# A decoder block in one fused kernel: first rows ahead of the constants, SSM turn factors moved into the attention, norm steps spread over the RW products, two units moved behind the gated product

## The reference

```python
def rms_norm(x, g):
    x32 = x.astype(jnp.float32)
    y = x32 * lax.rsqrt(jnp.mean(x32 * x32, axis=-1, keepdims=True) + EPS)
    return (y * g.astype(jnp.float32)).astype(x.dtype)
...
def diff_attention(q1, q2, k1, k2, v, lam):
...
        attn = probs(q1b, k1) - lam * probs(q2b, k2)
        return jnp.einsum('bhqk,bhkd->bhqd', attn, v32)
...
def s5_ssm(u, a_re, a_im, log_dt, b_re, b_im, c_re, c_im, d_skip):
```

## Time and profile before

| What | Value |
|---|---|
| Median of 3 runs | 3587.25 us (3585.57 to 3601.52) |
| Profiled execution, its time | 3581.31 us |
| Its span | 3579.3 us |
| Mean granted TensorE clock | 0.935 |
| Busy: PE, DVE, ACT, POOL | 87%, 49%, 24%, 55% |
| First product of the projection starts | 57.35 us |
| Projection ends, attention of half 0 begins | 218.5 and 243.6 us |
| glu(0) and the start of phase 1 | 548 to 604 us |
| mix_norm of half 1 in phase 2 | 1329 to 1362.7 us |

### The profile page before, as it was taken

One profiled execution on the slowest core, in us unless ns is written; L12 is line 12 of the kernel. 1 busy time (PEld: TensorE's weight loads), 2 busy tenths in 40 slices (PEclk: granted clock), 3 DMA queues, 4 the chain that ended last, 5 costly groups with the idle time before them and its releaser, 6 DMA issues.

```text
span 3579.3 us, 47875 instructions
## 1 busy us (share of the span) xinstructions
PE 3113.0 (87%) x19536; PEld 2394.1 (67%) x19536; DVE 1744.9 (49%) x2362; ACT 855.8 (24%) x1588; POOL 1969.1 (55%) x1076
## 2 busy tenths in 40 slices
PE   5977886699998768988999978988999989799997
PEld 4655564477776556766777766776777767688875
DVE  6733553443443552576666653286655564323233
ACT  3102112332222232122233223112222332200012
POOL 4801222255555464755676655665666674477873
PEclk9868997799999888999999999999999999899998
DMA  3334323122222233322222233432222221322331
GB/s 136 109 99 108 90 88 106 65 71 83 77 66 70 89 122 133 128 83 77 88 76 84 69 123 113 143 103 74 82 70 81 84 80 60 118 95 92 97 99 60
DMA packets 158027, 329.99 MB, mean 92 GB/s; under 512 B 34960, under 2 KB 74064, under 8 KB 157808
## 3 DMA queue, kind: packets, MB, share of 16 engines
q1 hardware_dynamic: 58752, 213.94, 18.6%
q10 hardware_dynamic: 99056, 112.99, 9.8%
HBM read 281.89 MB, written 44.97 MB: 91 GB/s over the span
## 4 chain that ended last, share of the span: by engine, by line
PE 71%; DVE 19%; ACT 3%; ACTq 2%; DMA 2%; issue 2%; DVEq 0%
PE ps L1778 30%; PE ps L1819 12%; PE ps L1807 12%; PE ps L1632 2%; DVE acc_dense L2219 2%; DVE ffh_lo L2903 1%; DVE act_lo L2219 1%; PE ps L1513 1%; DVE xn_dense L2226 1%; PE ps L2018 1%; ACTq L934 1%; PE ps L1553 1%; PE ps L1660 1%; DVE added L2219 1%; DVE turn L2219 1%
## 5 line engine op out<-in xcount | busy, mean ns | idle before, releaser
L537 POOL TENSOR_TENSOR w_hi<-w_raw,ones 128x1024 fp32r<-128x1024 f32 x408 | 795.0, 1949 | 1318.3 <-DMA w_raw<-weights 1304.3
L539 POOL TENSOR_TENSOR w_lo<-w_raw,w_hi 128x1024 fp32r<-128x1024 f32 x408 | 1006.6, 2467 | 32.0
L1778 PE MATMUL ps<-act_hi,w_hi 128*128 128x512 f32 x1696 | 702.6, 414 | 7.2 <-DVE act_lo L2219 6.6
L1778 PE MATMUL ps<-act_lo,w_hi 128*128 128x512 f32 x1696 | 676.7, 399 | 0.0
L1778 PE MATMUL ps<-act_hi,w_lo 128*128 128x512 f32 x1696 | 672.3, 396 | 0.0
L1778 PEld LDWEIGHTS ps<-act_hi,w_hi 128*128 128x128 f32 x1696 | 323.0, 190 | 99.1 <-issue 15.7
L1778 PEld LDWEIGHTS ps<-act_hi,w_lo 128*128 128x128 f32 x1696 | 322.8, 190 | 74.8
L1778 PEld LDWEIGHTS ps<-act_lo,w_hi 128*128 128x128 f32 x1696 | 322.8, 190 | 66.2 <-issue 1.7
L2219 DVE TENSOR_TENSOR acc_dense<-acc_dense,ps 128x512 f32<-128x512 f32 x352 | 242.0, 688 | 231.9 <-PE ps L1807 170.9
L1807 PE MATMUL ps<-w_hi,ffh_hi 128*128 128x512 f32 x704 | 293.7, 417 | 59.7 <-DVE acc_dense L2219 56.2
L1807 PE MATMUL ps<-w_hi,ffh_lo 128*128 128x512 f32 x704 | 279.7, 397 | 0.0
(11 more groups left out here) (374 smaller groups left out, 4482.9 us busy)
## 6 DMA issues: line engine op xcount, KB each, us to landing
w_raw<-weights SPq DMA_DIRECT2D x408, 512.0 KB, 3.5
rw<-rw_t ACTq DMA_DIRECT2D x24, 256.0 KB, 2.4
rw<-lora_t ACTq DMA_DIRECT2D x24, 256.0 KB, 2.0
row<-x ACTq DMA_DIRECT2D x8, 512.0 KB, 3.5
row_dense<-x ACTq DMA_DIRECT2D x8, 512.0 KB, 3.7
res<-row_dense ACTq DMA_DIRECT2D x8, 512.0 KB, 2.6
row_mix<-res ACTq DMA_DIRECT2D x8, 512.0 KB, 7.4
res<-row_mix ACTq DMA_DIRECT2D x8, 512.0 KB, 2.9
```

The costliest lines, as they stand in the source:

```text
L537: pool.tensor_tensor(w_hi[:, s], raw, ones[:, 0:1].to_broadcast([P, 1024]), MUL).then_inc(w_hi_made, 1)
L539: pool.tensor_tensor(w_lo[:, s], raw, w_hi[:, s].bitcast(F32), SUB).then_inc(w_ready, 1)
L1778: mm = pe.matmul(out, ws[w][:, s, P * k:P * k + P], acts[a][:, k, x], start=(k, w, a) == (0, 0, 0), stop=(k, w, a) == (KT - 1, 1, 0))
```

## The change

Six things change.

1. At the start ACT issues the first three rows and the gain ahead of the constants; `load_ssm` moves behind the third norm step, the lambda value and the SSM exponent behind the first norm; SP waits for the five constants before its first weight.
2. `double_frames` becomes `more_frames` and leaves the projection: three SSM steps `("frames", 0..2)` at attention steps 1, 3 and 5, the last doubling in two halves; the store is issued at the third. Attention(0)'s loads no longer wait for it, `load_input_factors(0)` does. The table and its scratch have other places in SBUF.
3. `rotated` writes its product back into PSUM, so that the third operation reads PSUM and SBUF.
4. The last two far units (nine pieces) come behind attention steps 66 and 67, behind the gated product of half 0, and their weights behind the GLU's.
5. Phase 1: the last four steps are followed by 12, 8, 4 and the rest of the chunks, four fewer ahead of them.
6. Phase 2: `mix_norm`'s six steps move out of the residual norm to behind RW tiles 0, 2, 4, 6, 8 and 10 (before: none there). Phase 3: `dense_norm`'s six steps move from behind tiles 0 to 5 to behind the same even tiles. `rw_t` and its neighbours lie 16 KB further on, off `acc_mix`.

```diff
-    SSM_STEPS = [("states", 0), ("states", 1), ("tables", 0), ("outputs", 0)]
+    SSM_STEPS = [("frames", n) for n in range(3)] + [("states", 0), ("states", 1), ("tables", 0), ("outputs", 0)]
...
-    rw_t = place("rw_t", [P, 2, BANK], F32, AT_MIX)
+    rw_t = place("rw_t", [P, 2, BANK], F32, AT_MIX + 16384)
...
-        return [ahead] + spread(through - ahead, ATT_STEPS - 1) + [8, 4, 4, rest - through - 16]
-
-    FILLS = {1: fills_heads(8, 8 * HALF + NORM_STEPS + 224, len(first_starts)),
-             2: fills([10, 8, 6, 6, 4, 4], [0] * RW_TILES, len(first_starts)),
+        return [ahead] + spread(through - ahead, ATT_STEPS - 1) + [12, 8, 4, rest - through - 24]
+
+    FILLS = {1: fills_heads(8, 8 * HALF + NORM_STEPS + 220, len(first_starts)),
+             2: fills([8, 8, 6, 6, 4, 0], [1, 0] * NORM_STEPS + [0] * (RW_TILES - 2 * NORM_STEPS), len(first_starts)),
...
-        at = [12, 14, 15] + [18 + 3 * n for n in range(2 * TB - 2)]
-        gated = (60, 63, 65, 67)
+        at = [1, 3, 5, 12, 14, 15] + [18 + 3 * n for n in range(2 * TB - 2)]
+        gated, ahead = (60, 63, 65, 67), FAR_PIECES - 9
...
+            elif n < gated[1]:
+                now = 8 + 2 * early + (ahead - 8 - 2 * early) * (n + 1 - early) // (gated[1] - early)
+            else:
+                now = min(FAR_PIECES, ahead + 5 * max(0, n - gated[2]))
...
+        sp.wait_ge(const_landed, 16 * 5)
         for pos, (_, u) in enumerate(ORDER):
...
-            if m == 0:
-                act.wait_ge(tables_stored, 16 * (3 * TB + 2))
...
         def load_input_factors(b):
+            if b == 0:
+                act.wait_ge(tables_stored, 16 * (3 * TB + 2))
...
+                elif kind == "frames":
+                    if b == 2:
+                        store_frames()
...
-                act.wait_ge(tables_stored, 16 * (3 * TB + 2))
+                act.wait_ge(tables_stored, 16 * 3 * TB)
...
+        for n in range(3):
+            load_row(0, n)
+        act.dma_start(gain_first[:, :], t["pre_mix_g"].partition_broadcast(P)).then_inc(gain_landed, 16)
         load_consts()
-        load_ssm()
+        table_for(ACT.Ln)
+        take(arg_ready)
+        first_norm()
         lambda_value()
...
-            tt(rope_sin_part[:, 0:c1 - c0], ps[:, bank, 0:c1 - c0], rope[:, 1, c0:c1], MUL)
+            tt(ps[:, bank, 0:c1 - c0], ps[:, bank, 0:c1 - c0], rope[:, 1, c0:c1], MUL)
             tt(qk_raw[:, m % 2, c0:c1], qk_raw[:, m % 2, c0:c1], rope[:, 0, c0:c1], MUL)
-            tt(qk_raw[:, m % 2, c0:c1], qk_raw[:, m % 2, c0:c1], rope_sin_part[:, 0:c1 - c0], ADD, rope_done)
+            tt(qk_raw[:, m % 2, c0:c1], ps[:, bank, 0:c1 - c0], qk_raw[:, m % 2, c0:c1], ADD, rope_done)
...
-        def double_frames(n):
+        def more_frames(have, n, first=1):
...
-                    for n in (1, 2, 4, 8, 16, 32):
-                        double_frames(n)
-                else:
-                    double_frames(64)
...
+                elif kind == "frames":
+                    for have, n, first in (((1, 1, 1), (2, 2, 1), (4, 4, 1), (8, 8, 1), (16, 16, 1)), ((32, 32, 1),), ((64, 32, 1), (64, 32, 33)))[b]:
+                        more_frames(have, n, first)
```

More of the change, by code:

```diff
@@ L194, in build @@
     turn = place("turn", [P, 2, 2, TQ, STATES], F32, ARENA + 29024)
-    frames = place("frames", [P, 2, PAIRS, STATES], F32, ARENA)
-    frame_tmp = place("frame_tmp", [P, 2, PAIRS * 64], F32, ARENA + 16640)
+    frames = place("frames", [P, 2, PAIRS, STATES], F32, ARENA + 16640)
+    frame_tmp = place("frame_tmp", [P, 2, PAIRS * 32], F32, ARENA + 12480)
     tables_at = {}
@@ L324, in build @@
     gain_post_mix = (place("gain_post_mix", [P, D], F32, AT_KEEP), gain_dense)
-    rw_t = place("rw_t", [P, 2, BANK], F32, AT_MIX)
[L327 to L331, removed]
+    rw_t = place("rw_t", [P, 2, BANK], F32, AT_MIX + 16384)
+    lora_t = place("lora_t", [P, 2, BANK], F32, AT_MIX + 20480)
+    wa = place("wa", [P, BANK], F32, AT_MIX + 24576)
+    sgd = place("sgd", [P, BANK], F32, AT_MIX + 26624)
+    lora_w = place("lora_w", [P, 4 * P], F32, AT_MIX + 28672)
+    lora_g = place("lora_g", [P, 4 * P], F32, AT_MIX + 30720)
     before_half = place("before_half", [P, RW_TILES], F32, AT_KEEP + 4096)
@@ L488, in head_events @@
         events, done, early = ["heads"] + ["far"] * 8, 8, 14
[L489 to L490 removed]
+        at = [1, 3, 5, 12, 14, 15] + [18 + 3 * n for n in range(2 * TB - 2)]
+        gated, ahead = (60, 63, 65, 67), FAR_PIECES - 9
         for n in range(ATT_STEPS - 1):
[L492 removed]
+            if n < early:
+                now = 8 + 2 * (n + 1)
+            elif n < gated[1]:
+                now = 8 + 2 * early + (ahead - 8 - 2 * early) * (n + 1 - early) // (gated[1] - early)
+            else:
+                now = min(FAR_PIECES, ahead + 5 * max(0, n - gated[2]))
             events += ["heads"] + ["far"] * (now - done) + ["ssm"] * at.count(n) + ["glu"] * gated.count(n)
@@ L498, in build @@
     HEAD_EVENTS = head_events()
-    ORDER = [(0, u) for u in range(U_V, U_GLU)] + [(0, u) for u in range(U_V)] + [(1, u) for u in range(U_V, U_GLU)] + [(0, U_GLU), (0, U_GLU + 1)]
+    ORDER = [(0, u) for u in range(U_V, U_GLU)] + [(0, u) for u in range(U_V)] + [(1, u) for u in range(U_V, U_GLU - 2)] + [(0, U_GLU), (0, U_GLU + 1), (1, U_GLU - 2), (1, U_GLU - 1)]
     EVENTS, PHASE_START = {}, {}
@@ L705, in first_norm @@
                     load_row(0, step + 1)
+                if step == 3:
+                    load_ssm()
         def lambda_value():
             table_for(ACT.Exp)
-            take(arg_ready, 2)
+            take(arg_ready)
             give(fn(small[:, 130:132], small[:, 128:130], ACT.Exp), fn_ready)
@@ L2453, in octet_turn @@
             give(dve.memset(frames[:, 1, :, 0:1], 0.0), dve_step)
-            give(dve.memset(xs[:, :, :, :, 0:1], 0.0), dve_step)
             tt(frames[:, 0, :, 1], w(4), w(5), MUL)
             tt(frames[:, 1, :, 1], w(3), w(5), MUL)
-        def double_frames(n):
+        def more_frames(have, n, first=1):
             wide = lambda v: v.unsqueeze(2).to_broadcast([P, PAIRS, n])
             tmp = frame_tmp[:, :, 0:PAIRS * n].rearrange("p a (q h) -> p a q h", h=n)
-            cmul(frames[:, 0, :, n + 1:2 * n + 1], frames[:, 1, :, n + 1:2 * n + 1], wide(frames[:, 0, :, n]), wide(frames[:, 1, :, n]),
-                 frames[:, 0, :, 1:n + 1], frames[:, 1, :, 1:n + 1], tmp[:, 0], tmp[:, 1], last=factors_ready if n == 64 else dve_step)
+            new, old = slice(have + first, have + first + n), slice(first, first + n)
+            cmul(frames[:, 0, :, new], frames[:, 1, :, new], wide(frames[:, 0, :, have]), wide(frames[:, 1, :, have]),
+                 frames[:, 0, :, old], frames[:, 1, :, old], tmp[:, 0], tmp[:, 1], last=factors_ready if have + first + n == STATES else dve_step)
         def build_factors(b):
@@ L2480, in turn_back_and_scan @@
             dve.wait_ge(factors_landed, 32 * (b + 1))
+            if b == 0:
+                give(dve.memset(xs[:, :, :, :, 0:1], 0.0), dve_step)
             dve.wait_ge(ssm_s, b + 1)
```

12 lines of the change are left out of this document (3 added, 9 removed).

## The result

The changed kernel takes 3604.61 us in the median of eight runs (3598.36 to 3616.34), against 3587.05 us before. The ratio is 1.0048, with a 95% interval of 1.0029 to 1.0067. It is slower by some 17 us, where I forecast 22 to 24 us faster.

A forecast was written before the change was run, and what follows sets the result against it. PE's work was taken as the floor, with gains only where PE waits or runs at half clock. The terms -9 -27 -6 +3 -3 -6 +30 -4 gave -22 on 3581.3, or 3559; with 4 us of offset 3563 us, range 3530 to 3592.

The forecast's parts named there:

- Part 1: Start: first row issued first, so the first `xn` comes 11 to 12 us sooner; net -9 us (-3 to -12).
- Part 2: Projection: doublings leave (-23 us) and rotations read PSUM (-4); together -27 us, between -18 and -34.
- Part 3: Frame store: attention's loads no longer wait for it, so PE's wait for `u_t` shrinks; -6 us (-5 to -8).
- Part 4: Frame doublings in the attention: first two lie beside far pieces, the third costs +3 us (0 to +10).
- Part 5: Nine far pieces behind glu(0): cover waits there, though the Q/K store comes later; -3 us (-7 to +4).
- Part 6: Tail of phase 1: four more chunks behind glu(1)'s steps, where PE waits; -6 us (-2 to -9).
- Part 7: Spaced norms in phase 2: four waits for `xn_dense` between RW products outweigh the earlier start; +30 us (+15 to +40).
- Part 8: Phase 3's `dense_norm`: spacing takes the table load's share of the first wait; -4 us (-5 to 0).
- A: Rival: phase 2's norms are hidden as in phase 3, -19 us in place of +30; 3514 us; chance 0.12.
- B: Rival: POOL paces the projection, which gives only 8 us; total -3, 3582 us; chance 0.13.
- D: Rival: the start gains nothing and the frames' third step costs +10 us; total -6, 3579 us; chance 0.09.
- C: Rival: clock stays low between phase 2's waits, adding 52 us in place of 10; total +20, 3605 us; chance 0.06.

The follow-up runs named there:

- the late turns: Changed kernel with PE turning, in each norm step of phase 2, the row made ready one step earlier than before: 3572.94 us, ratio 0.9941 to the kernel before.
- d2_norm3_back: Changed kernel with far pieces and phase 1's table restored, PE's phase 2 turns one step later, phase 3's norm behind tiles 0 to 5: 3544.41 us, ratio 0.9866.

## Why the prediction was wrong

The range held neither the sign nor the time (3604.61 against 3530 to 3592). By its own steps, in the traces:

- **Part 1, start**: -10.1, forecast -9. Right.
- **Part 2, projection**: -23.9, forecast -27. Right in sum, with the shares wrong: the rotations gave 7.7 alone and not 4, which leaves some 16 and not 23 for the doublings. I had let POOL's 28.35 busy us of 30 stand for a pace that held the rotations too, and I had let PE do the rest at full clock, where its last window is at 0.75.
- **Part 3, store**: -7.2, forecast -6. Right.
- **Part 4, frames**: +6.1, forecast +3; between 2.6 and 6.5 in the six other kernels with this part that have a wait for `u_t` to measure from. Right in direction.
- **Part 5, nine far pieces: the step that failed.** I wrote that they "cover waits such as 3.86 us at 577.25" and took -3, with +4 as the worst. The traces show 26.6 us of loss from the second attention turn to the first keys in this pair and about 20 over all kernels, and the whole kernel gains 25 us when they go back. Two errors made it. First, I priced the pieces only where they arrive. Where they left, they stood between attention steps whose turns wait for the chain over DVE and ACT; there the 53 matmuls ran for nothing, and without them idle time rose by 11 us and the clock fell. Second, I took "behind the gated product" for "under its waits". PE's list has them behind the squares' waits, which stayed at 3.37 and 3.47, and so their 14 us are added whole. The later Q/K store, which I had named as the risk, is not where it went: the wait for the keys does not follow the pieces.
- **Part 6, tail**: +10 in its stretch, +8 by the whole kernel's ratio, forecast -6. The second step that failed, in the same way: chunks behind waits are not under them, and I had not asked where they came from. Four of the eight came from under DVE's GLU work, and the last wait grew by the 5 us that they take. The split between the two halves of the table is read from the trace; I tested only the table as a whole.
- **Part 7, spaced norms in phase 2**: +26.4 from the last wait behind glu(1) to the first retention turn, and 31 us by the whole kernel, forecast +30. The waits were forecast as 9.0, 14.6, 14.6 and 6.8 and measured as 9.02, 14.77, 14.83 and 8.15. This was read from the order and the durations alone, and the late turns show that it was the cause.
- **Part 8, phase 3**: -4.8 in this pair, forecast -4; `d2_norm3_back` shows the first wait at 6.53 without it and 3.37 with it. Only these 3 us are clear: the stretch as a whole differs by some 10 us between kernels that have the same phase 3.
- Between phase 2's retention and phase 3 the changed kernel lost another 5 us (+27.4 to +32.3), which no part had. It is within what single executions differ by: that stretch is 606.4 us here and 598.9 to 611.0 in the other traces.

Of the rivals, A, B and D did not come (the start gained its 10 us). C, the one on the slower side, gave 3605, but that it meets the measured time is luck: the clock was back at 1.00 within 5 us behind a wait of 14.77, and the four waits with all that hangs on them cost 26.4 in place of the 72 that C needs. The mechanism that decided was not in the list. With part 5 at +25 and part 6 at +8 in place of -3 and -6, the same sum gives about +20, against 17.6 measured.

## What to carry to other kernels

Work moved to fill a wait must be priced twice: where it arrives, and where it leaves, since what ran free under somebody's latency may leave only idle time and a lower clock. Both tables failed here on the second price. On engines with a fixed order, "behind" is not "under": find the waiting instruction in the list and ask whether the moved work stands ahead of it. Here spacing the steps hid the latency only once the consumer's instruction also stood a step later than the producer's; an edit of three lines that moved PE's turn by a step was worth 38 us, where the spacing without it cost 31.

## What was not expected of the hardware

Behind the 14.77 us wait in phase 2 PE was back at full clock within five microseconds: 0.62 in the mean from 1394 to 1399, then 1.00. A DVE addition of two SBUF tensors took 1956 ns in the mean over the projection, six of eight between 1.11 and 2.73 us and two 0.69, and the same addition with one operand in PSUM 0.69 us in all eight cases. I had priced it from one long row and counted five rotations. But the time that it loses went in part to DVE's other operations on two SBUF tensors, as said above.

```profile
1394.00:1399.00 5.00, 4.81 (x18) 4.22 (x19) 1.51 (x3) 0.00 (x0) 0.00 (x0) 0.62 0.00 0
1399.00:1404.00 5.00, 5.00 (x20) 3.26 (x19) 0.53 (x2) 0.69 (x1) 0.00 (x0) 1.00 0.10 16
```
